# Two of the four heads' memory keys made in the first steps of the self-attention, and the copies of its high parts issued behind the turned probabilities

## Chip, cores and metric

The kernel is a hand-scheduled program for one core of a Trainium2 chip. It uses the core's five engines and its 16 DMA engines: PE (TensorE, matrix products; PEld is its weight load), DVE (VectorE), ACT (ScalarE), POOL (GpSimd) and SP (SyncE, which here only issues DMAs). The metric is the device time of one execution in microseconds (us), as the median of the runs; every number below that has no unit beside it is in us.

## The reference

One decoder layer over 1024 positions of width 1024, with 256 memory tokens:

```
x <- LN(alpha*x + mixer(x))          mixer = [retention | spatial gating | latent attention] @ w_out
x <- LN(alpha*x + cross(x, mem))     4 heads of 128, 256 memory tokens
x <- LN(alpha*x + moe(x))            16 experts, top 2 of one group

def memory_cross_attention(x, mem, wq, wk, wv, wo):
    q = (x @ wq).reshape(b, s, 4, 128)
    k = (mem @ wk).reshape(b, 256, 4, 128)      # the memory keys: they do not depend on x
    v = (mem @ wv).reshape(b, 256, 4, 128)
    p = softmax(q k^T * 128 ** -0.5)
    return (p v).reshape(b, s, 512) @ wo
```

The self-attention inside the mixer has 8 heads of 96 (64 without position, 32 rotated), values of 64, a causal mask, and works on 1024 keys.

## The kernel before

The program is a row of phases, each a block in which every engine has its own hand-written list of instructions. Engines meet only through semaphores inside a block, and all of them wait for one another at its end. The phases are `project` (the input projection), `prepare` (retention, gating, keys and queries of the self-attention), `attend` (the self-attention), `mix_out` (output projection, first normalization, memory keys), `cross_attend`, `experts` and `overflow`. A float32 product on PE is issued as two passes, so 8 products of one memory-key head show as 16 records. Where precision is bought more cheaply, an operand is split into a high part (type f32r) and a rest, and three products of one pass replace the two passes: names with `_hi` and `_lo`.

**prepare** (L435 to L658) walks over 8 tiles of 128 positions. PE turns the latents of the next tile (`latents_T`, L454 to L461, whose last transpose raises `lat_t`) inside the tile before. SP has nothing to do in this block.

**attend** (L667 to L902) works on 48 units, listed in `units` (L681): for tiles 0 to 3 a unit is two heads of a tile (4 units for a tile), for tiles 4 to 7 it is one head (8 units for a tile). Each unit u goes through this chain:

- PE `scores(u)` (L727 to L740) into half u % 2 of the buffer `s_ps`. Tiles 0 to 2 use plain float32 (L735); tiles from SPLIT = 3 on use three products of high and low parts (L737 to L739).
- DVE adds the causal mask (L853) and takes the row maximum (L857, L859).
- ACT exponentiates into `prob` (L805, L808).
- PE `turn(u)` transposes the probabilities into `t_ps` (L748).
- DVE copies the first half of them to `prob_T` (L866), ACT the second half (L817).
- PE `values(u)` multiplies them with the values (L761).

PE's order is `scores(u)`, `values(u-2)`, `turn(u-1)` for each u (L765 to L771). ACT's order for each u is: an eventual copy of high parts, then the exponentials of u, then the `prob_T` copy of u-1. The copies of high parts are `keys_high` (L776 to L780, 1024 columns of `k_hi`) and `queries_high` (L782 to L785, `q_hi`). For tiles 0 to 3 they stand ahead of units 4, 5, 6, 8 and 9 (L787 to L792); later, those of tile i+1 stand ahead of the units of heads 2 and 4 of tile i (L793 to L797). POOL makes the low parts from them (`k_lo` L876 and L889, `q_lo` L881), and `scores` of the first unit of a tile waits for both (L732 to L733). DVE also ends the retention at the start of its step u = 2 (L838, L842), and the high parts of the keys wait for that, since they are put where the retention's inputs were.

SP in attend (L706 to L714) loads slices 6 and 7 of `w_out` at once into a place of their own (62 KiB), then writes zeros into two DRAM tables (44 stores), then loads slices 0 to 5 of `w_out` to 137 KiB as the low parts of the queries that lie there are done with.

**mix_out** (L909 to L1063) multiplies the mixed heads with `w_out`, in three products of high and low parts (L975 to L977), adds x and normalizes. ACT splits `w_out` at tile 1, after waiting for all eight slices (L992 to L994). When the last tile's product is out, the block ends like this. PE makes the memory keys of all four heads, 8 products of 128x256 for each (L980 to L986). ACT makes the high part of the query weights (L1003). DVE adds the last tile (L1033), takes its statistics (L1037, L1039), normalizes the last two tiles (L1021, L1022), makes the low part of the query weights (8 subtractions, L1045) and copies the keys of four heads out of PE's buffer into `xkT` (4 copies, L1048). Then the block ends, and **cross_attend** starts with transposes (L1172), the memory values (L1288), and the queries (L1183 to L1185).

```
            n = len(units)
            for u in range(n + 2):
                if u < n: scores(u)
                if 0 <= u - 2: values(u - 2)
                if 0 <= u - 1 < n: turn(u - 1)
```

Of the kernel before, what the change touches and what calls it, by code (L numbers as in the profile page):

```python
# [15 lines left out]
P = 128  # L16
# [44 lines left out]
W_OUT_EARLY = 6  # L61
# [338 lines left out]
def prepare(nc, k):  # L400
# [266 lines left out]
def attend(nc, k):  # L667
# [25 lines left out]
    ret_normed, ret_gated = k.sem("ret_normed"), k.sem("ret_gated")  # L693
    k_hi_made, q_hi_made, q_lo_made, k_lo_made, k_old_lo_made = (
# [3 lines left out]
    nc.clear_and_free_semaphores([s for s in k.used[:older] if s is not k.ret_rstd_ready])  # L698
    with nc.psum_tensor("s_ps", [P, 2, 2, 512], f32) as sps, \
# [5 lines left out]
        def _(sp):  # L705
            for s in range(W_OUT_EARLY, KD):  # L706
                sp.dma_start(k.w_out_raw[s], A["w_out"][s * P:(s + 1) * P, :]).then_inc(k.w_out_loaded, 16)
# [4 lines left out]
            for s in range(W_OUT_EARLY):  # L712
                sp.wait_ge(scored, units.index((s + 1, 0)))
                sp.dma_start(k.w_out_raw[s], A["w_out"][s * P:(s + 1) * P, :]).then_inc(k.w_out_loaded, 16)  # L714
# [7 lines left out]
        def _(pe):  # L722
            def scores(u):
                i = units[u][0]
                if u >= 2:
                    pe.wait_ge(exps, 2 * (u - 1))
                if i == SPLIT:  # L727
                    pe.wait_ge(k_old_lo_made, units[u][1] // 2 + 1)
# [35 lines left out]

            n = len(units)  # L765
            for u in range(n + 2):
                if u < n:
                    scores(u)
                if 0 <= u - 2:
                    values(u - 2)  # L770
                if 0 <= u - 1 < n:  # L771
                    turn(u - 1)

        @block.scalar
        def _(act):
            def keys_high(t):  # L776
                if t == 0:
                    act.wait_ge(ret_gated, 1)
                tok = slice(t * P, (t + 1) * P)
# [7 lines left out]
            early = {4: 0, 5: 1, 6: 2, 8: SPLIT}  # L787
            for u in range(len(units) + 1):
                if u in early:
                    keys_high(early[u])  # L790
                if u == 9:
                    queries_high(SPLIT)  # L792
                if u < len(units) and SPLIT <= units[u][0] < NT - 1:  # L793
                    if units[u][1] == 2:
                        keys_high(units[u][0] + 1)
                    if units[u][1] == 4:
                        queries_high(units[u][0] + 1)  # L797
# [13 lines left out]
                if u >= 1:  # L811
# [5 lines left out]
                    act.activation(probT[:, v % 2, 1, 0:(z - a) * P], tps[:, 1, 0:(z - a) * P], ACT.Copy).then_inc(pT_copied_act, 1)  # L817

# [86 lines left out]
def mix_out(nc, k):  # L905
# [26 lines left out]
    with nc.psum_tensor("mixT_ps", [P, 2, 2, 512], f32) as tps, \  # L932
# [19 lines left out]
        def _(pe):  # L952
# [29 lines left out]
            for u in range(XH):  # L982
# [1177 lines left out]
```

## Time and profile before

| | |
|---|---|
| median of 3 runs | 1040.03 us (1038.56 to 1045.7) |
| the profiled execution, its own time | 1042.29 us |
| its span, first to last instruction | 1040.5 us |
| busy PE / PEld / DVE / ACT / POOL | 94% / 81% / 58% / 35% / 22% |
| granted TensorE clock, mean | 0.98 of full speed |

The profile shows one execution. Busy time of PE is modelled and includes waits inside its pipeline, so the start times of its instructions are the better measure. Between the first and the last instruction lie 1040.5 us, and 1.8 us of the execution's own time lie around them. "xN" after an instruction is a run of N records merged; the bracket behind it is the idle time of the engine before it and what ended it.

### The profile page before, as it was taken

Reading aid. Unit: us, or ns where it says so; the run is one execution under the profiler, and the core shown is the slowest. Engines: PE = TensorE matmul, PEld = TensorE weight load, DVE = VectorE, ACT = ScalarE, POOL = GpSimd, SP = SyncE. Lnnn points to the kernel's source line nnn. Section 1 sums busy time; section 2 is a strip of 40 time slices with the busy share of each in tenths; the row PEclk is TensorE's granted clock in tenths of the full one; section 3 lists DMA queues with packets and bytes.
Section 4 is the critical chain, followed back from the end, with each engine's and each line's share of the span. In section 5 each row is a group of like instructions: output and inputs, shape, how many; then the busy total and the mean of one; then the engine's idle time right before and its main releaser. Section 6 shows DMA issues by size and latency. Waiting matters only on the chain. (4 is left out here: it accounts for less than half of the span.)

```text
span 1040.5 us, 15996 instructions
## 1 busy us (share of the span) xinstructions
PE 981.2 (94%) x5687; PEld 843.9 (81%) x5687; DVE 607.8 (58%) x1273; ACT 365.8 (35%) x749; POOL 225.2 (22%) x286
## 2 busy tenths in 40 slices
PE   7999999999899999899999999999899999999993
PEld 5898877676779999778885888888778988888882
DVE  6644340677666665544472455458546676767674
ACT  5122131434564444500013332331134444544441
POOL 0012100121061110012220000003334544333343
PEclk9999999999799999899999999999899999999997
DMA  8022010000798100460203200042688788989962
GB/s 331 17 82 81 1 62 1 1 2 1 290 412 321 38 2 2 161 243 1 81 0 124 81 1 1 1 153 108 238 253 278 260 302 291 310 292 316 318 247 85
DMA packets 63737, 150.49 MB, mean 145 GB/s; under 512 B 10304, under 2 KB 12608, under 8 KB 63680
## 3 DMA queue, kind: packets, MB, share of 16 engines
q1 hardware_dynamic: 54720, 132.77, 36.3%
q0 software_dynamic: 8960, 16.96, 4.4%
q8 instruction: 36, 0.59, 0.2%
q14 instruction: 21, 0.17, 0.1%
HBM read 109.46 MB, written 54.92 MB: 158 GB/s over the span
## 5 line engine op out<-in xcount | busy, mean ns | idle before, releaser
L1764 PEld LDWEIGHTS h_ps<-xgT,e_gate_up 128*128 128x128 f32 x1024 | 157.2, 193 | 4.6 <-issue 2.3
L1764 PE MATMUL h_ps<-xgT,e_gate_up 128*128 128x176 f32 x1024 | 158.6, 317 | 2.2 <-PEq L1753 2.2
L248 PE MATMUL unit_ps<-whi,xhi 128*128 128x512 f32 (+1 forms) x256 | 98.3, 384 | 9.6 <-DVE wlo L279 9.6
L249 PE MATMUL unit_ps<-wlo,xhi 128*128 128x512 f32 (+1 forms) x256 | 98.0, 383 | 0.0
L250 PE MATMUL unit_ps<-whi,xlo 128*128 128x512 f32 (+1 forms) x256 | 97.9, 382 | 0.0
L761 PEld LDWEIGHTS o_ps<-mla_v,prob_T 128*128 128x128 f32 x576 | 71.5, 196 | 10.0 <-issue 5.2
L761 PE MATMUL o_ps<-mla_v,prob_T 128*128 128x64 f32 x576 | 72.7, 277 | 4.2 <-ACT prob_T L817 4.2
L248 PEld LDWEIGHTS unit_ps<-whi,xhi 128*128 128x128 f32 x256 | 48.7, 190 | 18.1 <-DVE xlo L318 7.4
L1882 DVE SCALAR_TENSOR_TENSOR z<-y_ps,slot_weight,x_rows 128x512 f32<-128x512 f32 (+1 forms) x64 | 45.6, 746 | 19.5 <-PE y_ps L1778 12.1
L1828 ACT ACTIVATE ln_junk<-z,z_neg_mean 128x1024 f32<-128x1024 f32 (+1 forms) x32 | 36.8, 1150 | 54.8 <-DVE z_neg_mean L1887 54.3
L1776 PE MATMUL y_ps<-e_dn_hi,h_hi 128*128 128x512 f32 (+1 forms) x128 | 52.1, 407 | 4.1 <-DVE z L1882 4.1
L250 PEld LDWEIGHTS unit_ps<-whi,xlo 128*128 128x128 f32 x256 | 48.6, 190 | 7.7
L249 PEld LDWEIGHTS unit_ps<-wlo,xhi 128*128 128x128 f32 x256 | 48.6, 190 | 7.6
L975 PE MATMUL mix_acc<-wo_hi,mixT_hi 128*128 128x512 f32 x128 | 51.1, 399 | 3.4 <-DVE wo_lo L1027 2.1
L976 PE MATMUL mix_acc<-wo_lo,mixT_hi 128*128 128x512 f32 x128 | 50.6, 395 | 0.0
L977 PE MATMUL mix_acc<-wo_hi,mixT_lo 128*128 128x512 f32 x128 | 50.5, 395 | 0.0
L1778 PE MATMUL y_ps<-e_dn_hi,h_lo 128*128 128x512 f32 (+1 forms) x128 | 50.5, 395 | 0.0
L1777 PE MATMUL y_ps<-e_dn_lo,h_hi 128*128 128x512 f32 (+1 forms) x128 | 50.2, 392 | 0.0
L808 ACT ACTIVATE prob<-s_ps,neg_max 128x640 f32<-128x640 f32 (+3 forms) x32 | 30.5, 954 | 55.5 <-issue 53.9
L866 DVE COPY prob_T<-t_ps 128x512 f32<-128x512 f32 (+3 forms) x48 | 29.9, 624 | 25.1 <-PE t_ps L748 25.0
L1850 DVE SCALAR_TENSOR_TENSOR ln_out<-ln_tmp,z_rstd,ln_b 128x1024 f32<-128x1024 f32 (+1 forms) x34 | 42.0, 1277 | 4.3 <-POOL z_rstd L1730 4.3
L1733 POOL DMA_INDIRECT out<-ln_out,slot_ids x32 | 34.0, 1062 | 46.4 <-DVE ln_out L1850 41.5
(313 smaller groups left out, 2093.0 us busy)
## 6 DMA issues: line engine op xcount, KB each, us to landing
e_gate_up<-w_gu SPq DMA_DIRECT2D x16, 2048.0 KB, 11.7
e_down_raw<-w_dn SPq DMA_DIRECT2D x16, 1024.0 KB
slot_rows<-zeros SPq DMA_DIRECT2D x22, 522.0 KB, 7.1
slot_sums<-zeros SPq DMA_DIRECT2D x22, 512.0 KB, 7.3
x_rows<-slot_rows SPq DMA_DIRECT2D x16, 522.0 KB, 4.4
slot_sums<-z SPq DMA_DIRECT2D x16, 512.0 KB, 4.0
wraw<-w_in SPq DMA_DIRECT2D x24, 256.0 KB, 4.7
xraw<-xT SPq DMA_DIRECT2D x8, 512.0 KB, 7.1
```

The lines of the kernel that those rows point to most:

```text
L248: pe.matmul(o, hi, whi[:, s, 0:w], start=(s == 0), stop=False)
L249: pe.matmul(o, hi, wlo[:, s, 0:w], start=False, stop=False)
L250: last = pe.matmul(o, lo, whi[:, s, 0:w], start=False, stop=(s == KD - 1))
L761: last = pe.matmul(ops[:, i % 2, h * MV:(h + 1) * MV], probT[:, u % 2, j, (m - a) * P:(m - a + 1) * P], k.v[:, m, h * MV:(h + 1) * MV], st ...
L975: pe.matmul(o, hi, whi[:, s, c], start=(s == 0), stop=False)
L976: pe.matmul(o, hi, wlo[:, s, c], start=False, stop=False)
L977: last = pe.matmul(o, lo, whi[:, s, c], start=False, stop=(s == KD - 1))
L1764: end = pe.matmul(hps[:, m, gu * CAP:(gu + 1) * CAP], gate_up[:, b, s, w], xT[:, s, :], start=(s == 0), stop=(s == KD - 1))
L1776: pe.matmul(out, hi, dn_hi[:, b, w, :], start=(f == 0), stop=False)
L1777: pe.matmul(out, hi, dn_lo[:, b, w, :], start=False, stop=False)
L1778: return pe.matmul(out, lo, dn_hi[:, b, w, :], start=False, stop=(f == 1))
L1882: dve.scalar_tensor_tensor(z[c][:, f], yps[r, BANK[u], :], wgt[r, b, c:c + 1], rows[b][r, c, f], ALU.mult, ALU.add, accum_out=zsum[r, c, j ...
```

## The change

- Head 0 and head 1 of the memory keys are made in attend: PE's list starts with `scores(0)`, `early_keys(0)`, `turn(0)`, `scores(1)`, `early_keys(1)`, `values(0)`, `turn(1)`, `scores(2)`, and goes on in the old order from u = 3 (where `scores(3)` comes first). ACT copies each result to `xkT`. `scores(1)` and `scores(2)` wait for these copies.
- Their inputs (1 MB of `memT`, two 512 KB column blocks of `xa_wk`) are loaded by SP in prepare, once the latents of the last tile are turned.
- mix_out makes and copies heads 2 and 3 only. It still loads all of `memT` and `xa_wk`.
- In attend, ACT's copies of high parts stand behind the exponentials and the `prob_T` copy of their step. For tiles 0 to 3 the step is one less than before; for the later ones it is the same step.
- All slices of `w_out` go to 137 KiB, slices 6 and 7 too; slice 7 is loaded when all scores are done. `xkT` is moved to another address.

```
-W_OUT_EARLY = 6
+KEYS_EARLY = 2
...
+        @block.sync
+        def _(sp):
+            sp.wait_ge(lat_t, NT)
+            sp.dma_start(k.mem_early[:], A["memT"].rearrange("(s p) n -> p s n", p=P)).then_inc(k.early_loaded, 16)
+            wk = A["xa_wk"].rearrange("(s p) n -> p s n", p=P)
+            for h in range(KEYS_EARLY):
+                sp.dma_start(k.wk_early[h][:], wk[:, :, h * XD:(h + 1) * XD]).then_inc(k.early_loaded, 16)
...
-            for s in range(W_OUT_EARLY, KD):
-                sp.dma_start(k.w_out_raw[s], A["w_out"][s * P:(s + 1) * P, :]).then_inc(k.w_out_loaded, 16)
...
-            for s in range(W_OUT_EARLY):
-                sp.wait_ge(scored, units.index((s + 1, 0)))
+            for s in range(KD):
+                sp.wait_ge(scored, units.index((s + 1, 0)) if s + 1 < NT else len(units))
...
+                if 1 <= u <= KEYS_EARLY:
+                    pe.wait_ge(keys_taken, u)
+            def early_keys(h):
+                if h == 0:
+                    pe.wait_ge(k.early_loaded, 16 * (1 + KEYS_EARLY))
+                else:
+                    pe.wait_ge(exps, 2 * h)
+                for s in range(KD):
+                    last = pe.matmul(sps[:, 1 - h, 0, 0:MEM], k.wk_early[h][:, s, :], k.mem_early[:, s, :], start=(s == 0), stop=(s == KD - 1))
+                last.then_inc(keys_sum, 1)
-            for u in range(n + 2):
+            scores(0)
+            early_keys(0)
+            turn(0)
+            scores(1)
+            early_keys(1)
+            values(0)
+            turn(1)
+            scores(2)
+            for u in range(3, n + 2):
...
                 if t == 0:
                     act.wait_ge(ret_gated, 1)
+                    act.wait_ge(keys_taken, KEYS_EARLY)
-            early = {4: 0, 5: 1, 6: 2, 8: SPLIT}
+            early = {3: 0, 4: 1, 5: 2, 7: SPLIT}
             for u in range(len(units) + 1):
-                if u in early:
-                    keys_high(early[u])
-                if u == 9:
-                    queries_high(SPLIT)
-                if u < len(units) and SPLIT <= units[u][0] < NT - 1:
...
+                if u < KEYS_EARLY:
+                    act.wait_ge(keys_sum, u + 1)
+                    act.activation(k.xkT[:, u, :], sps[:, 1 - u, 0, 0:MEM], ACT.Copy).then_inc(keys_taken, 1)
+                if u in early:
+                    keys_high(early[u])
+                if u == 8:
+                    queries_high(SPLIT)
+                if u < len(units) and SPLIT <= units[u][0] < NT - 1:
...
...
-            for u in range(XH):
+            for u in range(KEYS_EARLY, XH):
```

## Rows read from the trace of the kernel before

**Rows 1.** The page's part 1: busy time, share, instructions.
```profile
PE 981.2 (94%) x5687; PEld 843.9 (81%) x5687; DVE 607.8 (58%) x1273; ACT 365.8 (35%) x749; POOL 225.2 (22%) x286
```
**Rows 2.** Windows: stretch, length, busy PE PEld DVE ACT POOL, PEclk, DMA share, GB/s.
```profile
265.30:268.70 3.40, 1.16 (x9) 1.00 (x9) 1.91 (x5) 1.44 (x6) 1.27 (x2) 0.98 0.42 128
268.70:282.20 13.50, 12.85 (x49) 11.31 (x50) 6.70 (x18) 8.07 (x28) 0.00 (x0) 0.50 1.01 405
...
435.60:439.10 3.50, 3.50 (x11) 2.68 (x10) 3.50 (x4) 3.50 (x5) 0.00 (x0) 0.53 1.01 413
...
530.70:544.40 13.70, 13.70 (x65) 11.96 (x63) 12.70 (x17) 4.27 (x8) 2.71 (x2) 1.00 0.00 1
```
**Rows 3.** Timeline, end of mix_out and start of cross_attend.
```profile
530.73 13.97 PE L984 MATMUL mixT_ps<-memT,xa_wk_raw 128*128 128x256 f32 x64
...
531.00 1.22 DVE L1033 SCALAR_TENSOR_TENSOR x<-x,mix_acc 128x1024 f32<-128x1024 f32 x1 [5.70 <-PE mix_acc L977]
...
539.41 4.90 DVE L1045 TENSOR_TENSOR wq_lo<-wq_raw,wq_hi 128x512 fp32r<-128x512 f32 x8
544.24 1.41 DVE L1048 COPY xkT<-mixT_ps 128x256 f32<-128x256 f32 x4
...
545.95 1.06 PE L1172 MATMUL x_tps<-constants,x 128*128 128x128 f32 x8 [1.25 <-PEq L934]
...
546.85 7.03 PE L1288 MATMUL x_acc<-xa_wv_raw,memT 128*128 128x512 f32 x16
```
**Rows 4.** Timeline, end of prepare and first units of attend.
```profile
253.12 0.27 PE L461 MATMUL banks<-constants,kr 128*32 128x128 f32 x1
...
266.17 1.13 PE L735 MATMUL s_ps<-mla_kT,mla_qT 96*128 96x128 f32 x8 [1.30 <-PEq L450]
...
268.67 0.69 PE L748 MATMUL t_ps<-constants,prob 128*128 128x128 f32 x2 [1.38 <-ACT prob L805]
...
274.20 1.91 PE L735 MATMUL s_ps<-mla_kT,mla_qT 96*128 96x256 f32 x4
...
282.36 0.43 DVE L853 TENSOR_TENSOR s_ps<-s_ps,constants 128x256 f32<-128x256 f32 x1 [1.71 <-PE s_ps L735]
...
282.83 0.69 DVE L857 TENSOR_REDUCE neg_max<-s_ps 128x2 f32<-128x512 f32 x1
...
283.45 1.03 PE L735 MATMUL s_ps<-mla_kT,mla_qT 96*128 96x256 f32 x4
...
284.46 0.38 ACT L817 ACTIVATE prob_T<-t_ps 128x256 f32<-128x256 f32 x1
...
286.34 1.46 PE L735 MATMUL s_ps<-mla_kT,mla_qT 96*128 96x384 f32 x4
```
**Rows 5.** Timeline, end of attend and start of mix_out.
```profile
418.59 0.39 PE L739 MATMUL s_ps<-k_hi,q_lo 96*128 96x512 f32 x1
...
432.28 5.78 ACT L994 ACTIVATE wo_hi<-w_out_head 128x1024 fp32r<-128x1024 f32 x6
...
434.92 0.47 PE L975 MATMUL mix_acc<-wo_hi,mixT_hi 128*128 128x512 f32 x1 [2.14 <-DVE wo_lo L1027]
```
**Rows 6.** Timeline, the last units of tile 3.
```profile
307.70 1.05 ACT L785 ACTIVATE q_hi<-mla_qT 96x1024 fp32r<-96x1024 f32 x1
...
308.83 2.36 POOL L881 TENSOR_TENSOR q_lo<-mla_qT,q_hi 96x1024 fp32r<-96x1024 f32 x1 [1.06 <-ACT q_hi L785]
...
310.06 0.69 ACT L805 ACTIVATE prob<-s_ps,neg_max 128x512 f32<-128x512 f32 x1 [1.31 <-DVE neg_max L857]
...
311.40 0.59 ACT L817 ACTIVATE prob_T<-t_ps 128x512 f32<-128x512 f32 x1
...
314.74 0.48 PE L737 MATMUL s_ps<-k_hi,q_hi 96*128 96x512 f32 x1
```
**Rows 7.** DMA issues: x count, KB each, median us to landing.
```profile
w_out_head<-w_out SPq DMA_DIRECT2D x6, 512.0 KB, 7.7
...
memT<-memT SPq DMA_DIRECT2D x1, 1024.0 KB, 5.5
```

More of the change, by code:

```diff
@@ L696, in attend @@
     on, mv4, rs4, ret_ps = k.ret_last
-    nc.clear_and_free_semaphores([s for s in k.used[:older] if s is not k.ret_rstd_ready])
+    nc.clear_and_free_semaphores([s for s in k.used[:older] if s is not k.ret_rstd_ready and s is not k.early_loaded])
     with nc.psum_tensor("s_ps", [P, 2, 2, 512], f32) as sps, \
@@ L711, in _ @@
                 sp.dma_start(k.z_dram[t * P:(t + 1) * P, :], zeros[:, 0:D]).then_inc(k.rows_zeroed, 16)
[L712 to L714 removed]
+            for s in range(KD):
+                sp.wait_ge(scored, units.index((s + 1, 0)) if s + 1 < NT else len(units))
+                sp.dma_start(k.w_out_raw[:, s, :], A["w_out"][s * P:(s + 1) * P, :]).then_inc(k.w_out_loaded, 16)
         def parts(u):
@@ L763, in values @@
                 last.then_inc(pv_done, 1)
-            n = len(units)
-            for u in range(n + 2):
+            def early_keys(h):
[6 more added lines that the diff above has]
+                last.then_inc(keys_sum, 1)
+            n = len(units)
+            scores(0)
[7 more added lines that the diff above has]
+            for u in range(3, n + 2):
                 if u < n:
                     scores(u)
-                if 0 <= u - 2:
-                    values(u - 2)
-                if 0 <= u - 1 < n:
+                values(u - 2)
+                if u - 1 < n:
                     turn(u - 1)
@@ L817, in _ @@
                     act.activation(probT[:, v % 2, 1, 0:(z - a) * P], tps[:, 1, 0:(z - a) * P], ACT.Copy).then_inc(pT_copied_act, 1)
+                if u < KEYS_EARLY:
[6 more added lines that the diff above has]
+                if u < len(units) and SPLIT <= units[u][0] < NT - 1:
+                    if units[u][1] == 2:
+                        keys_high(units[u][0] + 1)
+                    if units[u][1] == 4:
+                        queries_high(units[u][0] + 1)
         @block.vector
@@ L993, in _ @@
                     for s in range(KD):
-                        act.activation(whi[:, s, :], wraw[s], ACT.Copy).then_inc(w_hi, 1)
+                        act.activation(whi[:, s, :], wraw[:, s, :], ACT.Copy).then_inc(w_hi, 1)
                 act.wait_ge(mix_t, t + 1)
@@ L1045, in _ @@
                 dve.tensor_tensor(k.wq_lo[:, s, :], rawq[:, s, :], k.wq_hi[:, s, :].bitcast(f32), ALU.subtract)
-            for u in range(XH):
-                dve.wait_ge(keys_sum, u + 1)
+            for u in range(KEYS_EARLY, XH):
+                dve.wait_ge(keys_sum, u - KEYS_EARLY + 1)
                 dve.tensor_copy(k.xkT[:, u, :], tps[:, u // 2, u % 2, 0:MEM])
@@ L2076, in program @@
     k.v = at("mla_v", 169, [P, NT, MW])
-    k.w_out_tail, k.w_out_loaded = at("w_out_tail", 62, [P, KD - W_OUT_EARLY, D]), k.sem("w_out_loaded")
-    w_out_head = at("w_out_head", 137, [P, W_OUT_EARLY, D])
-    k.w_out_raw = [w_out_head[:, s, :] if s < W_OUT_EARLY else k.w_out_tail[:, s - W_OUT_EARLY, :] for s in range(KD)]
+    k.w_out_raw, k.w_out_loaded = at("w_out_raw", 137, [P, KD, D]), k.sem("w_out_loaded")
     k.wuq = at("w_uq", 192, [P, QR // P, MH * MQ])
@@ L2089, in program @@
     k.memT = at("memT", 73, [P, KD, MEM])
-    k.xkT, k.xv = at("xkT", 12, [P, XH, MEM]), at("xv", 16, [P, 2, XW])
+    k.xkT, k.xv = at("xkT", 6, [P, XH, MEM]), at("xv", 16, [P, 2, XW])
+    k.mem_early = at("mem_early", 60, [P, KD, MEM])
+    k.wk_early = [at(f"xa_wk_early{h}", (68, 52)[h], [P, KD, XD]) for h in range(KEYS_EARLY)]
+    k.early_loaded = k.sem("early_loaded")
     k.xs_dram = nc.dram_tensor("slot_rows", [SLOTS, ROW], f32).ap()
```

7 lines of the change are left out of this document (2 added, 5 removed).

## The prediction, made before any run of the change

> **What bounds the kernel now.** I read the page's busy shares first: PE is busy for 94% of the span, every other engine for 58% or less [rows 1]. So PE's list is the thing to shorten, and a product that is moved from one place to another gains only if PE has idle time in the new place and is what the old place waits for. The average can't say that, so I went to the two places: the windows for clock and busy time [rows 2], then the timeline of both [rows 3, 4].
>
> The old place is the end of mix_out [rows 3]. The last product with `w_out` is out at about 530.9. From there two engines work side by side until the block ends. PE makes the keys of four heads: 64 records from 530.73, the last one's end at 544.70. DVE adds, normalizes, makes the low part of the query weights until 544.31 (539.41 + 4.90) and copies four keys until 545.65 (544.24 + 1.41). In 13.7 us DVE is busy for 12.70 [rows 2], and its four copies start back to back with no wait before them. So PE and DVE end together, and PE's keys are not alone in setting the end. The reader is to see that 7 us less of PE's work leave 14.3 us of DVE's list as they are.
>
> The new place is the start of attend [rows 4]. PE idles for 1.30 before the first scores (the change of blocks) and for 1.38 before the first `turn`, which waits for mask, maximum and exponentials of unit 0. The granted clock tells something else about this place: full until 268.7, then 0.50, the lower of the two levels (1.2 against 2.4 GHz), until 282.2 [rows 2]. The same four passes of 128x256 scores take 1.91 at 274.20 and 1.03 at 283.45 [rows 4]. PE had 1.16 busy us in the 3.4 before the clock fell [rows 2].
>
> **The change part by part.**
>
> *Keys taken out of mix_out.* Two heads are 32 of 64 records: 13.97 / 2 = 7.0 off PE's list, which then ends at about 537.7. DVE loses two of four copies, (1.41 - 0.41) / 3 = 0.33 apart (0.41 is one copy, taken from this line's own duration), so 0.67. DVE ends at 544.98 instead of 545.65, and the block with it. Gain: 0.7. Cover: DVE's chain from 531.0 to 544.31 (12.70 busy of 13.70), and it doesn't hang on PE's keys. Bounds: 0.7 if DVE stays the last, 7.0 if it were not there.
>
> *What the idle PE then costs.* PE stands still from 537.7 to 545.3, 7.6 us, and has dense work from 545.95: 1.06 of transposes, then 16 records of the memory values, which are the way to the queries [rows 3]. I take what followed the idle time before 434.92, 2.14 of it: the clock was at 0.53 from 435.6 to 439.1 though PE was busy for all of it [rows 2, 5]. Half of 3.5 us is lost there, 1.7. Here I take 1.5, since the transposes in front count for less. Bounds: 0, and 3.5 if two such stretches follow.
> The Trainium skill speaks against this part of the change: "TensorE: Matmul & The Clock Gate", section "What's actually happening", says that throttled is the default state and that activity releases it. By that rule a PE with nothing to do is not free, and the keys at the end also served to keep the clock up. The row at 434.92 agrees; no row shows the end of mix_out with an idle PE. Without the rule's effect the sum would be 1.5 lower.
>
> *Keys put into attend.* Each head costs 3.5 on PE at full clock (13.97 / 4). I follow the units by the durations of rows 4 at full clock. `scores(0)` is done at 266.7. Keys 0 run to 270.2. The softmax of unit 0 (268.6) lies under them, so the 1.38 of idle time before the first `turn` is used. Then `turn(0)`; ACT copies key 0 (0.38, as the 128x256 copy at 284.46), `scores(1)` waits for that and starts at about 270.85 (0.25 idle). Keys 1 run from 271.4 to 274.9, and the softmax of unit 1 and the end of the retention on DVE lie under them. `values(0)`, `turn(1)`, `scores(2)` to 276.3, `scores(3)` to 276.8. Now PE's order bites: `values(1)` stands behind `scores(3)` but needs ACT's `prob_T` copy of unit 1, which ACT makes after the exponentials of unit 2, and those need `scores(2)` of just before. Mask and maximum to 277.25, exponentials to 278.1, copy to 278.4: PE idles for 1.7. `scores(4)` starts at 279.15, where it was 274.20: 4.95 late.
> Then the steps run at full clock where they ran at half. At full clock a step is held by the chain scores, maximum, exponentials, `prob_T` copy, not by PE: 2.89 from 283.45 to 286.34. At half clock the four steps from 274.20 to 286.34 took 12.14, of which the last two were in part already at full clock. At full clock I take two steps as one turn of the chain: mask and maximum 1.15, two exponentials with their reads 1.3, copy 0.38, `values`, `turn` and `scores` on PE 2.0, handovers 0.2: 5.0, so 10.0 for four, and 1.0 for the `k_hi` copies of 1.05 that come in the way of exponentials: 11.0. So the lateness at `scores(8)` is 4.95 - 1.2 = 3.8. From there on the chain before and after is the same, and nothing in attend waits for a fixed time that could take it back: the zero stores have SP's queue to themselves and POOL's work hangs on the scores.
> Cost: 3.8. Bounds: 2.0 (all idle time in the first steps used, 1.38 + 1.3, and 2.3 from the clock) and 11 (below).
>
> *Clock in the new place.* I take it that the clock stays up: in place of 1.16 busy us in the stretch ahead of 268.7 PE would have about 2.5 of them, and dense ones. If it falls all the same, the keys are themselves the dense work that brought it back at 439.1 after 3.5 us.
>
> *Copies of high parts moved on ACT.* For tiles 0 to 3 "behind the copy of step u" and "ahead of step u + 1" is the same place in ACT's list, so nothing changes. For tiles 3 to 6 each copy of 1.05 moves from the front of its step to the back. It delayed nothing in front: ACT still idled before the next exponentials (1.31 before 310.06, behind the `q_hi` of 307.70) [rows 6]; so nothing is gained. What is late next is POOL's low part of the queries of tile 4. A tile of two-head units has only two steps between the copy and the next tile: now ACT does exponentials from 310.06, the `prob_T` copy until 311.99, then `q_hi` to 313.05; POOL needs 2.36 [rows 6], done at 315.45, where `scores` of tile 4 starts at 314.74. Stall: 0.7; the steps after it may take back some, as far as PE waits in them. I take 0.5. Later tiles have four steps between, and no stall. Bounds: 0 and 0.8.
>
> *Loads.* The latents of the last tile are turned at 253.4 [rows 4]. SP, idle in prepare, then issues three loads. `memT` with 1024 rows of 1 KB took 5.5 [rows 7]; two blocks of 1024 rows of 512 bytes lie between half of that and all of it each. One after the other the three are in at 264.4 to 269.9, and they overlap in part, since 5.5 holds the time to start too; the keys want them at 266.7. I cost this at nothing. The cover is the last tile of prepare (253.4 to 266.17); if it is gone, the keys start up to 3.2 late.
> The Trainium skill bears on this: "DMA: Bandwidth & Descriptors", section "Specifications", puts the smallest transfer for full rate at 512 bytes, which these rows just reach; no row of this case has that size. By it the loads come in early in the interval, and the sum is the same; only the chance of a late load is smaller.
> Slice 7 of `w_out` is now issued when the last scores are done, at 419.0, and takes 7.7 at most like its neighbours [rows 5, 7]: 426.7. ACT wants it at 432.28. Slack 5.6, cost nothing. The two 512 KB loads taken from the front of SP's list in attend don't bring the zero stores forward, as these wait for a memset. ACT's two key copies (0.38 each) are short, and only `scores(1)` waits for one with nothing else to do (the 0.25 above).
>
> **The sum.** 3.8 + 0.5 - 0.7 + 1.5 = 5.1 slower. The profiled execution had 1042.29 (span 1040.5), which gives 1047.4; against the median of the runs, 1040.03, it gives 1045.1, and this is my forecast. A measurement of this kernel can tell about 1% from no change (10.4 us), so half a per cent is "the same".
>
> **The rivals.**
> 1. *The clock stays down in the early steps* (slower side). The change of blocks leaves 1.30 idle, and PE's gaps behind keys 0 and keys 1 (0.25, 1.7) are like those that came with the fall at 268.7. Then both heads cost double, 7.0 more, and the later steps gain nothing back, 1.2 less: 1045.1 + 8.2 = 1053.3. It decides from the point where the clock is at half before keys 1 start. For it: 13.5 us at half clock now in this very place. Against: dense work ended the other low stretch within 3.5 us.
> 2. *The end of mix_out really gains* (faster side). If DVE's list were shorter than it looks, or its rows waited for PE in a way the profile hides, 7.0 would come off instead of 0.7, and with no idle PE there no clock is lost: 1045.1 - 6.3 - 1.5 = 1037.3. Against: DVE is busy for 12.70 of 13.70 there.
> 3. *The early keys cost little.* They fill idle time of the softmax chain at lower cost than I find (2.0 instead of 3.8), and the clock at the end holds: 1045.1 - 1.8 - 1.5 = 1041.8.
> 4. *The change doesn't find its inputs*: the loads come late, PE idles in front of keys 0 for up to 3.2, and the clock falls on that: 3.2 + 1.7, 1050.0.
>
> **How the numbers follow.** Forecast 0.55, rival 1 0.14, rival 2 0.07, rival 3 0.17, rival 4 0.07. The forecast's own range is 1041 to 1049 (its bounds and a run-to-run spread of some us). To hold 8 of 10 the range takes in rivals 3 and 4 and reaches to rival 1: 1038 to 1053. Over 1% slower is above 1050.4: most of rival 1 and a little of the rest, 0.13. Over 1% faster is below 1029.6: no case reaches it, 0.02. Same: 0.85.
>
> **What would show it.** In the changed profile: DVE's subtractions of `wq_lo` still end some 14.3 after the last tile's product, and the block ends 0.7 sooner than now by that count, with PE idle for about 7 us before the transposes of cross_attend. The granted clock is below full in the first 3 to 4 us of the memory values. In attend the keys are 16 records each, 0.22 apart, and the clock is at full through 268 to 282; `scores(3)` is followed by an idle PE until ACT's copy of unit 1; the first `scores` of tile 3 comes about 3.8 later than now; at the first unit of tile 4 PE waits for `q_lo`. Wrong would be: keys 0.43 apart, keys waiting for a DMA, a DVE that idles before `xkT`, or an attend that is not longer than now.

## The result and the profile after

The change costs about half a per cent: 1047.12 us in the median of 20 runs (1043.41 to 1053.1) against 1041.55 (1037.91 to 1047.89) for the kernel before, run beside it. The ratio is 1.0045, with a 95% interval of 1.0029 to 1.006; that is 4.7 us slower (the two medians are 5.6 apart), where the forecast was 5.1, and it lies within the 1% that the prediction called "the same". Of all the runs behind this document one is left out of its ratio, a run of e1 that took 1187 us at a granted clock of 0.80.

The profiled execution of after is the slowest of its 20, with an own time of 1053.1 (span 1051.0). So the stages are compared one by one, and only those that the change touches are put down to it. I cut the span at starts of products on PE, read from the timelines:

```
stage (from .. to)                                    before    after    difference
A  first scores .. first scores of tile 3              33.00    37.21      +4.21
B  .. last scores (tiles 3 to 7)                      119.42   119.69      +0.27
C  .. first product with w_out                         16.33    16.33       0.00
D  .. last product with w_out                          95.58    95.31      -0.27
E  .. first transposes of cross_attend                 15.45    14.80      -0.65
F  .. first query product                               7.37    10.35      +2.98
G  .. end of cross_attend's work, start of placement  178.35   178.19      -0.16
H  .. first expert product                             17.31    16.54      -0.77
   .. end of the span (experts)                       291.52   296.08      +4.56
```

A, B, E and F are where the change works, and they hold 6.8. The 4.56 in the experts is not the change's: the profiles of the ten experiments, which leave the experts as they are, have from 287.0 to 293.5 there with no relation to their edit. What makes that part vary is open. G ends, and H begins, at PE's second group of placement products (`x_qps<-selected_b`). The page's first part says little, as before [rows 1]: PE's busy time and its count of records are the same, since the products have only moved.

```profile
PE 982.1 (93%) x5687; PEld 841.3 (80%) x5687; DVE 607.4 (58%) x1271; ACT 366.8 (35%) x751; POOL 225.8 (21%) x286
```

The windows say more (stretch, length, busy PE, PEld, DVE, ACT, POOL, granted clock, DMA share, GB/s). The first four are the start of attend and answer to the first two of [rows 2]; the last three are the end of mix_out with PE busy, then with PE idle, and the start of cross_attend.

```profile
265.30:268.70 3.40, 2.20 (x12) 2.05 (x13) 1.47 (x3) 1.42 (x5) 1.61 (x2) 1.00 0.00 0
268.00:279.00 11.00, 9.11 (x53) 7.78 (x52) 4.41 (x14) 4.05 (x19) 0.12 (x1) 1.00 0.93 379
279.20:286.00 6.80, 6.80 (x27) 5.80 (x26) 3.16 (x7) 4.23 (x12) 0.00 (x0) 0.52 1.02 418
286.30:304.00 17.70, 16.58 (x110) 13.23 (x109) 11.87 (x22) 11.08 (x32) 11.52 (x6) 1.00 1.02 412
...
535.30:542.40 7.10, 7.04 (x33) 5.86 (x31) 6.23 (x7) 4.27 (x8) 2.71 (x2) 1.00 0.00 0
542.40:549.50 7.10, 0.00 (x0) 0.00 (x0) 7.03 (x12) 0.00 (x0) 0.00 (x0) 0.73 0.00 1
549.80:556.20 6.40, 6.36 (x14) 3.68 (x15) 1.23 (x1) 1.02 (x1) 1.01 (x7) 0.52 0.84 301
```

Before, 13.5 us at the start of attend were at half clock. Now the clock is full through both keys, and half only from 279.2 to about 286. At the end of mix_out PE is idle for 7.1 us in which DVE is busy for 7.03: DVE's list is what the block still has to wait for. The 6.4 us behind the change of blocks are at half clock.

The timeline of after at the start of attend (start, duration, engine, line, operation, out<-in, shape, records; in the bracket the idle time before it and what ended it), beside [rows 4]:

```profile
266.50 0.68 PE L744 MATMUL s_ps<-mla_kT,mla_qT 96*128 96x128 f32 x4 [1.31 <-PEq L450]
...
267.02 3.62 PE L781 MATMUL s_ps<-mem_early,xa_wk_early 128*128 128x256 f32 x16
...
271.11 0.71 PE L744 MATMUL s_ps<-mla_kT,mla_qT 96*128 96x128 f32 x4 [0.26 <-ACT xkT L838]
...
271.66 3.62 PE L781 MATMUL s_ps<-mem_early,xa_wk_early 128*128 128x256 f32 x16
...
275.84 1.13 PE L744 MATMUL s_ps<-mla_kT,mla_qT 96*128 96x128 f32 x8
...
278.61 0.63 PE L770 MATMUL o_ps<-mla_v,prob_T 128*128 128x64 f32 x4 [1.64 <-ACT prob_T L835]
...
279.30 1.79 PE L744 MATMUL s_ps<-mla_kT,mla_qT 96*128 96x256 f32 x4
...
303.71 0.47 PE L746 MATMUL s_ps<-k_hi,q_hi 96*128 96x512 f32 x1
```

The keys start 0.5 behind the first scores with no wait for a load, and 16 records take 3.62, 0.22 apart. There are two gaps, 0.26 for ACT's copy of key 0 and 1.64 in front of `values(1)`, and behind the second the scores take 1.79 instead of 1.03: that is half clock.

The end of mix_out and the start of cross_attend in after, beside [rows 3]:

```profile
535.27 7.07 PE L1014 MATMUL mixT_ps<-memT,xa_wk_raw 128*128 128x256 f32 x32
...
535.55 1.22 DVE L1063 SCALAR_TENSOR_TENSOR x<-x,mix_acc 128x1024 f32<-128x1024 f32 x1 [5.70 <-PE mix_acc L1007]
...
543.97 4.91 DVE L1075 TENSOR_TENSOR wq_lo<-wq_raw,wq_hi 128x512 fp32r<-128x512 f32 x8
...
548.79 0.75 DVE L1078 COPY xkT<-mixT_ps 128x256 f32<-128x256 f32 x2
...
549.84 1.94 PE L1202 MATMUL x_tps<-constants,x 128*128 128x128 f32 x8 [7.50 <-PEq L964]
...
551.57 9.19 PE L1318 MATMUL x_acc<-xa_wv_raw,memT 128*128 128x512 f32 x16
...
560.19 0.80 PE L1213 MATMUL x_qps<-wq_hi,x1T_hi 128*128 128x512 f32 x1
```

From DVE's addition to the end of its list are 13.99 us (549.54 - 535.55); before there were 14.65. PE has stood idle for 7.50 before the transposes, which then take 1.94 instead of 1.06, and the memory values 9.19 instead of 7.03.

### The profile page after: what moved, and what is told of

It is laid out like the page before. It is cut to its first block and busy times, and to the rows that moved or that the text cites. A ratio compares the mean times of both kernels' runs of the same rounds, so it can differ in the third digit from the quotient of the medians.

```text
span 1051.0 us, 16001 instructions
## 1 busy us (share of the span) xinstructions
PE 982.1 (93%) x5687; PEld 841.3 (80%) x5687; DVE 607.4 (58%) x1271; ACT 366.8 (35%) x751; POOL 225.8 (21%) x286
## 5 line engine op out<-in xcount | busy, mean ns | idle before, releaser
L1794 PEld LDWEIGHTS h_ps<-xgT,e_gate_up 128*128 128x128 f32 x1024 | 154.7, 191 | 4.7 <-issue 2.5
L1794 PE MATMUL h_ps<-xgT,e_gate_up 128*128 128x176 f32 x1024 | 156.1, 313 | 2.2 <-issue 2.2
```

The lines of the kernel that those rows point to most:

```text
L1794: end = pe.matmul(hps[:, m, gu * CAP:(gu + 1) * CAP], gate_up[:, b, s, w], xT[:, s, :], start=(s == 0), stop=(s == KD - 1))
```

## The experiments

Each ran beside the kernel before on the same chip, 12 runs in five rounds; e1 to e4, e5 to e8, and e9 with e10 ran on three different chips, so only the ratios to the kernel before can be compared, not the times. Differences to after are differences of such ratios, each known to 2 or 3 us, so that 1 or 2 us between two kernels are not told apart by time. Where the time can't tell, the stage lengths of the profiles help, in single executions. They scatter too wherever the clock falls in one execution and not in another, by 1 or 2 us, so a stage length counts only where rows of the timeline explain it:

```
kernel                    ratio [95%]               A      B      E      F      G     own time
before                                            33.00  119.42  15.45   7.37  178.35  1042.29
after                     1.0045 [1.0029,1.0060]  37.21  119.69  14.80  10.35  178.19  1053.10
e1_tail_short             1.0005 [0.9979,1.0030]  32.30  119.39  15.46  10.07  178.20  1038.62
e2_tail_filled            1.0012 [0.9988,1.0037]  37.20  119.77  14.79   7.37  179.92  1042.78
e3_copies_in_front        1.0048 [1.0028,1.0068]  35.20  119.36  14.79   8.96  178.61  1045.59
e4_keys_behind_scores2    1.0022 [1.0000,1.0043]  33.39  119.80  14.79  10.14  177.39  1042.27
e5_values_in_tail         1.0008 [0.9987,1.0029]  36.14  119.75  15.09   3.44  177.31  1036.46
e6_all                    0.9987 [0.9961,1.0013]  33.39  119.40  15.09   3.44  179.92  1039.22
e7_pool_takes_half        1.0055 [1.0032,1.0077]  35.19  119.78  16.20   9.94  176.17  1045.99
e8_only_copies_moved      1.0004 [0.9980,1.0028]  34.25  119.79  15.46   7.37  177.65  1039.81
e9_values_split           0.9965 [0.9940,0.9990]  33.38  119.38  15.09   3.43  175.21  1034.94
e10_tail_empty            0.9993 [0.9975,1.0011]  32.89  119.44  14.93   9.09  177.64  1036.60
```

**e1_tail_short: only the removal.** In before, mix_out's PE makes heads 2 and 3 alone.

```
-            for u in range(XH):
+            for u in range(2, XH):
                 for s in range(KD):
                     last = pe.matmul(tps[:, u // 2, u % 2, 0:MEM], ...
...
-                dve.wait_ge(keys_sum, u + 1)
-                dve.tensor_copy(k.xkT[:, u, :], tps[:, u // 2, u % 2, 0:MEM])
+                dve.wait_ge(keys_sum, u % 2 + 1)
+                dve.tensor_copy(k.xkT[:, u, :], tps[:, 1, u % 2, 0:MEM])
```

> The kernel before, with PE's products for memory keys 0 and 1 left out at the end of mix_out (32 of 64 records, 7.0 us of PE); DVE still makes four copies, of heads 2 and 3 twice, so the keys of heads 0 and 1 are not computed. Theory (DVE sets the end, and the idle PE loses clock): the block ends when it did, and the memory values behind it run partly at half clock, so 1.5 to 3 us slower than before. Rival (PE's products set the end): 6 to 7 us faster than before. Second rival (DVE sets the end, the idle time is free): no change, within 0.5 us.

Measured: 1039.7 against 1040.19, ratio 1.0005. That 7 us of PE's work at the end of mix_out are worth 7 is excluded (at most 2.2 faster); of the expected 1.5 to 3 slower the time shows nothing. Windows and timeline of e1:

```profile
536.00:544.00 8.00, 0.05 (x1) 0.00 (x0) 7.83 (x14) 0.00 (x0) 0.00 (x0) 0.72 0.00 1
544.20:551.00 6.80, 6.79 (x16) 3.96 (x17) 1.22 (x1) 1.02 (x1) 0.98 (x7) 0.59 0.85 308
```
```profile
542.49 1.41 DVE L1048 COPY xkT<-mixT_ps 128x256 f32<-128x256 f32 x4
...
544.21 1.94 PE L1172 MATMUL x_tps<-constants,x 128*128 128x128 f32 x8 [8.16 <-PEq L934]
```

DVE's list goes on as if nothing had been taken away: its four copies take the same 1.41, and the block ends with them (E 15.46, before 15.45). Behind the idle 8.16 the clock is at 0.59 and F is 2.70 longer. The time doesn't show these 2.7, which leaves open how much of a clock loss seen in a profile reaches the median; the interval allows it (up to +3.1).

**e10_tail_empty: all four heads out.** In before, no memory key is made at all; DVE copies raw weights in their place.

```
-            for u in range(XH):
-                for s in range(KD):
-                    last = pe.matmul(tps[:, u // 2, u % 2, 0:MEM], ...
-                last.then_inc(keys_sum, 1)
...
-                dve.tensor_copy(k.xkT[:, u, :], tps[:, u // 2, u % 2, 0:MEM])
+                dve.tensor_copy(k.xkT[:, u, :], k.wk[:, u, 0:MEM])
```

> The kernel before with all 64 records of the memory keys left out at the end of mix_out (14 us of PE); DVE copies four blocks of the raw weights in their place, so no memory key is computed. Theory (DVE's list of 14.8 us sets the end, and idle time costs one stretch of half clock however long it is): no faster than the kernel before, and up to 3 us slower; the block ends at most 0.5 us sooner after the last product with w_out. Rival (PE's products take part in setting the end): 7 to 14 us faster.

Measured: 1036.68 against 1037.7, ratio 0.9993. Fourteen us of PE's work are gone and nothing that can be measured is won. Timeline of e10:

```profile
531.04 1.22 DVE L1028 SCALAR_TENSOR_TENSOR x<-x,mix_acc 128x1024 f32<-128x1024 f32 x1 [5.70 <-PE mix_acc L977]
...
539.45 4.91 DVE L1040 TENSOR_TENSOR wq_lo<-wq_raw,wq_hi 128x512 fp32r<-128x512 f32 x8
...
544.27 0.90 DVE L1043 COPY xkT<-xa_wk_raw 128x256 f32<-128x256 f32 x4
...
545.47 1.94 PE L1167 MATMUL x_tps<-constants,x 128*128 128x128 f32 x8 [14.54 <-PEq L934]
```

DVE's rows are those of [rows 3] to within 0.04, only the copies are shorter (0.90 for 1.41), with a PE that has stood idle for 14.54. E is 0.52 shorter than in before, and the copies are 0.51 shorter. So PE's keys have no part in setting this end; DVE's list has, with one wait of 0.52 in it, for POOL's `ln_rs`. In the profile the shorter E and the longer F make 1.2 more than before; the interval of the time ends at +1.1.

**e2_tail_filled: the change, with PE busy in the old place.** In after, mix_out's PE makes all four heads; those of heads 0 and 1 are used by nobody.

```
-            for u in range(KEYS_EARLY, XH):
+            for u in (2, 3, 0, 1):
```

> The changed kernel, but PE makes all four heads' keys in mix_out too (heads 0 and 1 again, uncopied), so PE is busy until DVE is done. Theory: 7 us of useless products make it 1.5 to 3 us faster than the changed kernel, since the memory values stay at full clock; in the trace the first query product comes 7.4 us after the block's start as in the kernel before, not 10.4. Rival (the slow stretch in the changed profile is chance): the same as the changed kernel, or slower.

Measured: 1042.52 against 1040.19, ratio 1.0012. So 7 us of useless products seem to make after faster, by about 3.4 (1.0045 - 1.0012); the intervals overlap, and by them the 3.4 could be anything from about 0.5 to 6, so the profile has to carry it. Windows and timeline of e2:

```profile
549.00:552.00 3.00, 2.82 (x13) 1.89 (x14) 0.66 (x1) 1.02 (x1) 1.01 (x7) 1.00 0.52 178
```
```profile
549.18 1.06 PE L1202 MATMUL x_tps<-constants,x 128*128 128x128 f32 x8 [0.59 <-PEq L964]
```

The transposes take 1.06 again and F is 7.37 to the hundredth, as in before. (Not all of this profile speaks for e2. C, where its edit changes nothing, is 15.45 instead of 16.33, and G is 1.73 longer than in after, since products near its end run 0.43 apart instead of 0.23: the granted clock is 0.50 from 714.0 to 719.5.) Here the trace agrees with the Trainium skill, "TensorE: Matmul & The Clock Gate", section "What's actually happening", by which the throttled clock is the default and activity releases it. The price of an idle PE is in every profile that has one in front of the values: F is longer by 2.98 in after, 1.59 in e3, 2.77 in e4, 2.57 in e7, 2.70 in e1 and 1.72 in e10. In the time it may show here; in those of e1 and e10 it doesn't.

**e3_copies_in_front: the moved copies put back.** In after, ACT's `keys_high` and `queries_high` stand ahead of the exponentials again.

```
-            early = {3: 0, 4: 1, 5: 2, 7: SPLIT}
+            early = {4: 0, 5: 1, 6: 2, 8: SPLIT}
             for u in range(len(units) + 1):
+                if u in early:
+                    keys_high(early[u])
...
                 if u < len(units):
                     i, h = units[u]
```

> The changed kernel with ACT's copies of high parts back in front of the exponentials of their step. Theory: PE's wait for the low part of the queries at tile 4 (0.46 us in the changed profile) is gone, 0.3 to 0.7 us faster than the changed kernel, and nothing else moves. Rival (the move behind takes 1.05 us copies out of the way of exponentials, and is a gain): 0.5 to 2 us slower than the changed kernel.

**e8_only_copies_moved: the moved copies alone.** In before, the same blocks stand behind the `prob_T` copy.

```
-            early = {4: 0, 5: 1, 6: 2, 8: SPLIT}
+            early = {3: 0, 4: 1, 5: 2, 7: SPLIT}
...
                     act.activation(probT[:, v % 2, 1, 0:(z - a) * P], ...).then_inc(pT_copied_act, 1)
+                if u in early:
+                    keys_high(early[u])
...
```

> The kernel before with only ACT's copies of high parts moved behind their step. Theory: PE waits for the low part of the queries at tile 4, and the stretch from the first unit of tile 3 to the last scores is 0.3 us longer (119.7 instead of 119.4); the whole is within 0.5 us of the kernel before. Rival (moving them behind clears the way for exponentials): 0.5 to 2 us faster than before.

Measured: e3 1045.44 against 1040.19 (1.0048), e8 1037.9 against 1037.32 (1.0004). Neither time shows an effect. The profiles do: B is 119.69 to 119.80 in all six kernels whose copies stand behind, and 119.36 to 119.44 in all six whose copies stand in front. Rows of after, then of e8, at the first unit of tile 4, which answer to [rows 6]:

```profile
316.41 1.05 ACT L812 ACTIVATE q_hi<-mla_qT 96x1024 fp32r<-96x1024 f32 x1
...
317.54 2.35 POOL L911 TENSOR_TENSOR q_lo<-mla_qT,q_hi 96x1024 fp32r<-96x1024 f32 x1 [1.79 <-ACT q_hi L812]
...
319.99 0.47 PE L746 MATMUL s_ps<-k_hi,q_hi 96*128 96x512 f32 x1 [0.46 <-issue]
```
```profile
317.70 0.47 PE L737 MATMUL s_ps<-k_hi,q_hi 96*128 96x512 f32 x1 [0.47 <-issue]
```

POOL's low part ends at 319.89 and the scores start 0.10 later, behind 0.46 of idle time. That idle time is put down to "issue", but what ended just before it is POOL's row. e8 has the same gap, 0.11 behind the end of POOL's `q_lo`, and in e3 `q_lo` is done 3.5 ahead of these scores and there is no gap. So this part costs 0.3 to 0.4 in the profile.

**e4_keys_behind_scores2: another order of the first steps.** In after, key 1 is made behind `scores(2)` instead of in front of it, in a bank of `o_ps`, so that ACT's chain for unit 2 can start while PE makes it. For that bank to be free, DVE ends the retention one step earlier.

```
             scores(1)
+            scores(2)
             early_keys(1)
             values(0)
             turn(1)
-            scores(2)
...
-                    last = pe.matmul(sps[:, 1 - h, 0, 0:MEM], ...
+                    last = pe.matmul(sps[:, 1, 0, 0:MEM] if h == 0 else ops[:, 1, 0:MEM], ...
...
-                if u == 2:
+                if u == 1:
                     end_retention()
```

> The changed kernel with key 1 put behind scores(2) instead of ahead of values(0) and scores(2), in another PSUM bank, and the end of the retention one DVE step earlier. Theory (the idle 1.64 us of PE before values(1) comes from scores(2) being late, and the fall of the clock at 279 comes from that idle time): the idle time is gone and the clock stays up through the first units, 1.4 to 3 us faster than the changed kernel. Rival (the early steps are held by the two keys' 7 us of PE alone): within 0.5 us of the changed kernel.

Measured: 1042.15, ratio 1.0022, which is some 2.4 less than after; the intervals overlap. Windows and timeline of e4:

```profile
265.50:299.00 33.50, 31.53 (x195) 25.64 (x195) 20.07 (x44) 19.54 (x63) 12.24 (x7) 1.00 0.95 383
```
```profile
270.17 1.16 PE L744 MATMUL s_ps<-mla_kT,mla_qT 96*128 96x128 f32 x8 [0.26 <-ACT xkT L841]
...
271.17 3.62 PE L781 MATMUL o_ps<-mem_early,xa_wk_early 128*128 128x256 f32 x16
...
275.86 0.63 PE L770 MATMUL o_ps<-mla_v,prob_T 128*128 128x64 f32 x4
...
276.56 1.03 PE L744 MATMUL s_ps<-mla_kT,mla_qT 96*128 96x256 f32 x4
```

The gap of 1.64 is gone, the clock is full through all of A, and A is 33.39: two heads' keys for 0.4 more than before has without them. In the order of the change they are 2.2 above before at full clock (35.20 in e3) and 4.2 in after. The earlier end of the retention is not what gains here: in after DVE was done with it and then stood idle for 2.15 until unit 2's scores came.

```profile
276.56 0.43 DVE L883 TENSOR_TENSOR s_ps<-s_ps,constants 128x256 f32<-128x256 f32 x1 [2.15 <-PE s_ps L744]
```

The 1.8 between e3 and e4 compares two kernels at full clock. The 0.4 and the 2.2 don't: before had 13.5 us of half clock in A, and the kernels without early keys range from 32.30 (e1, at half clock for some 10 us) to 34.25 (e8, for over 16). Part of what makes the keys look cheap is that this low stretch is gone with them; no run shows A without keys at full clock.

**e5_values_in_tail: useful work in the emptied place.** In after, `memory_values(0)`, which stood between the first transposes and the first queries, is made at the end of mix_out, and ACT copies it there, where DVE copied it at the start of cross_attend.

```
@@ mix_out
+            pe.wait_ge(taken, NT - 1)
+            for s in range(KD):
+                last = pe.matmul(acc[:, 0, 0, :], memT[:, s, 0:P], k.wv[:, s, :], start=(s == 0), stop=(s == KD - 1))
...
+            act.activation(k.xv[:, 0, :], acc[:, 0, 0, :], ACT.Copy)
@@ cross_attend
             turn(0)
-            memory_values(0)
```

> The changed kernel with the first half of the memory values (16 records, 6.9 us of PE) moved from the start of cross_attend into PE's idle time at the end of mix_out; ACT copies them. Theory (PE was idle there for 7.5 us, and that idle time cost half-clock time behind it): the block ends about 0.6 us later than in the changed kernel, the first query product comes 3.5 us after the transposes instead of 10.4, and the kernel is 5 to 6 us faster than the changed one, about as fast as the one before. Rival (work in cross_attend's start is filler that hides ACT's and DVE's splitting of x, so moving it only opens a hole): at most 1 us faster than the changed kernel.

Measured: 1038.34 against 1037.32, ratio 1.0008: 3.8 less than after, where 5 to 6 were expected. F falls from 10.35 to 3.44, and E rises by 0.3. Part of the 6.9 in F isn't seen in the time. The hole of which the rival spoke is there too: PE waits 2.37 for DVE's low part of x in front of the first query product, as in e6 below.

**e6_all: e4, e5 and the copies in front together.**

> The values moved as in e5_values_in_tail, key 1 behind scores(2) as in e4_keys_behind_scores2, and ACT's copies in front as in e3_copies_in_front. If the parts add up: 4.2 us of the first units fall to 0.4, the 0.3 us of tile 4 are gone, the start of cross_attend is 3.9 us shorter than before: 3 to 4 us faster than the kernel before. Rival (the gains overlap, or the clock takes them back elsewhere): no faster than the kernel before.

Measured: 1036.79 against 1037.32, ratio 0.9987, an interval that holds no change. It was expected to win by 3 to 4; by the interval that is about the most that it can be. Windows and timeline of e6:

```profile
549.20:555.40 6.20, 6.17 (x15) 4.82 (x16) 0.00 (x0) 0.00 (x0) 0.00 (x0) 0.50 1.03 332
```

```profile
549.23 0.79 PE L1223 MATMUL x_qps<-wq_hi,x1T_hi 128*128 128x512 f32 x1 [2.37 <-DVE x1T_lo L1448]
...
549.82 0.63 PE L1224 MATMUL x_qps<-wq_lo,x1T_hi 128*128 128x512 f32 x1
```

With the values gone, nothing lies between the transposes and the queries: PE waits 2.37 for DVE's low part of x, and the queries behind it run 0.63 each, at half clock. The 24 products of the first tile's queries lie 8.23 from first to last start (549.23 to 557.46), against 5.64 in before; G is 179.92, 1.6 more than before. So moving the values filled one hole and opened another.

**e9_values_split: that gap filled too.** e6, with three of the eight steps of `memory_values(1)` taken from behind the queries and put into the gap.

```
-            def memory_values(m):
-                for s in range(KD):
+            def memory_values(m, steps):
+                for s in steps:
...
             turn(0)
+            memory_values(1, range(3))
```

> As e6_all, and three of the eight steps (6 of 16 records, 2.6 us) of the second half of the memory values pulled forward to stand between the first transposes and the first queries of cross_attend, where e6_all left PE idle for 2.37 us and the queries behind it ran at half clock. Theory (that idle time cost 1.5 to 1.7 us of half clock): the first queries come 0.2 us later after the transposes, at full clock, and the stretch up to the placement is 4 us shorter than in e6_all; 1.5 to 4 us faster than e6_all, 3 to 6 us faster than the kernel before. Rival (the second half of the values is needed as filler where it stood): no better than e6_all.

Measured: 1032.87 against 1037.7, ratio 0.9965, interval 0.994 to 0.999: 3.6 faster than the kernel before (between 1.0 and 6.2), and 2.3 faster than e6, whose interval overlaps. It is the only kernel here whose interval lies below that of after and below no change. Timeline of e9:

```profile
545.59 1.06 PE L1212 MATMUL x_tps<-constants,x 128*128 128x128 f32 x8 [0.93 <-PEq L968]
...
546.49 2.74 PE L1328 MATMUL x_acc<-xa_wv_raw,memT 128*128 128x512 f32 x6
...
549.02 0.50 PE L1223 MATMUL x_qps<-wq_hi,x1T_hi 128*128 128x512 f32 x1
```

Six records of 0.46 each fill the gap, the queries start at the same distance from the transposes (F 3.43), the first now 0.50 long, and the 24 products of the first tile lie 5.36 apart (549.02 to 554.38), 2.9 less than in e6. G is 175.21, 4.7 less than in e6; some 2.6 of that are the six records that now stand in F instead.

**e7_pool_takes_half: DVE's list shortened.** In after, four of the eight subtractions of `wq_lo` go to POOL.

```
-            for s in range(KD):
+            for s in range(KD // 2, KD):
                 dve.wait_ge(q_hi, s + 1)
                 dve.tensor_tensor(k.wq_lo[:, s, :], ...
...
+            for s in range(KD // 2):
+                pool.wait_ge(q_hi, s + 1)
+                pool.tensor_tensor(k.wq_lo[:, s, :], rawq[:, s, :], k.wq_hi[:, s, :].bitcast(f32), ALU.subtract)
```

> The changed kernel with four of the eight subtractions of the query weights' low part given from DVE to POOL at the end of mix_out. Theory (DVE's list sets the end of the block): the block ends 2 to 2.5 us sooner after the last product with w_out, and the kernel is 1.5 to 2.5 us faster than the changed one. Rival (something else holds the end, or POOL beside DVE slows both): less than 0.5 us.

Measured: 1044.84 against 1037.32, ratio 1.0055. The block ends 1.4 later than in after (E 16.20 against 14.80) instead of sooner. Timeline of e7:

```profile
538.35 7.33 POOL L1096 TENSOR_TENSOR wq_lo<-wq_raw,wq_hi 128x512 fp32r<-128x512 f32 x4
...
538.48 2.21 DVE L1051 SCALAR_TENSOR_TENSOR ln_tmp<-x,ln_mv,ln_g 128x1024 f32<-128x1024 f32 x1 [0.52 <-POOL ln_rs L1093]
...
542.93 4.50 DVE L1075 TENSOR_TENSOR wq_lo<-wq_raw,wq_hi 128x512 fp32r<-128x512 f32 x4
```

Each engine pays for the other. DVE's normalizing row takes 2.21, where it took 1.28 in after, and four subtractions take 4.50, where eight took 4.91. POOL needs 1.83 for each of its four; alone it took 2.35 for the 1024 columns of `q_lo` in after, from which an estimate for 512 is 1.18. The expected gain of 1.5 to 2.5 was missed because of this, and the miss says nothing against DVE's list as what sets the end: POOL is done at 545.68, DVE at 548.10, and PE's transposes start at 548.40, 0.30 behind DVE as in after.

```profile
547.36 0.74 DVE L1078 COPY xkT<-mixT_ps 128x256 f32<-128x256 f32 x2
```

## Why the prediction was right, step by step

**What bounds the two places: right.** DVE's list sets the end of mix_out. It predicted 0.7 from two fewer copies, and E is 0.65 shorter; the rows of e1 and e10 show DVE's list unmoved by a PE that has half or none of its products there.

**Keys in attend, 3.8: the mechanism held, the two parts of its size came out otherwise.** The start was followed to the tenth: the gap before `scores(1)` 0.26 (0.25 predicted), the gap before `values(1)` 1.64 (1.7), and `scores(4)` at 279.30 (279.15). The four steps from `scores(4)` to `scores(8)` were put at 11.0 at full clock, where before took 12.14; that was too slow. In e3, where the clock held, they took 9.56 (278.73 to 288.29), so 2.6 of the lateness came back, not 1.2. And "the clock stays up" failed in the profile of after, against the sign that the prediction had named for it: the clock fell behind that gap of 1.64, from 279.2 to 286, and the four steps took 11.57. Five profiles with the change's order of PE's first steps say how firm this is: in after, e2 and e5 the clock fell (A 37.21, 37.20, 36.14), in e3 and e7 it didn't (35.20, 35.19). So the term is 2.2 where the clock holds and 3.1 to 4.2 where it doesn't, and the 3.8 that was taken lies among the latter; it was too dear for the case that it described. The time of e2, which is nearly the keys alone (1.0012, at most +3.8), fits the 2.2 better than the 4.2.

**Idle PE, 1.5: the mechanism held, the size was at the low end; 3.0 in the profile of after, 1.6 to 2.8 in others.** It was taken from the stretch behind an idle 2.14, where half of 3.5 us was lost [rows 2, 5]. Behind 7.5 idle us the low clock held through the transposes and most of the values: 0.88 more on the transposes (1.94 for 1.06) and 2.16 on the values (9.19 for 7.03), together 3.0, near the upper bound of 3.5. Where the prediction saw the clock below full in the first 3 to 4 us of the values, it was so from the transposes on for 6.4. Behind the same idle 7.5, F is only 1.6 longer in e3 and 2.8 in e4 (2.6 in e7, behind 8.91), so the price differs from one execution to the next. e2 brings F back to 7.37; the times of e1 and e10 show no such price in before, so the median's share of it stays uncertain.

**Copies behind, 0.5: right, 0.3 in the profile.** The wait is where it was put, at the first unit of tile 4, for POOL's `q_lo`.

**Loads, slice 7, ACT's two copies: right, nothing.** No wait of PE for a load or of ACT shows, except the 0.26 that was foreseen. The keys start at 267.02 with no idle time, and ACT's first split of `w_out` waits for nothing. The issues in SP's list and that split, in after's timeline and in its DMA table (x count, KB each, median us to landing):

```profile
253.75 0.38 SPq L456 DMA_DIRECT2D mem_early<-memT  x1
...
254.18 2.26 SPq L459 DMA_DIRECT2D xa_wk_early<-xa_wk  x2
...
423.82 0.33 SPq L721 DMA_DIRECT2D w_out_raw<-w_out  x1
...
437.09 7.67 ACT L1024 ACTIVATE wo_hi<-w_out_raw 128x1024 fp32r<-128x1024 f32 x8
```
```profile
mem_early<-memT SPq DMA_DIRECT2D x1, 1024.0 KB, 5.4
...
xa_wk_early<-xa_wk SPq DMA_DIRECT2D x2, 512.0 KB, 6.7
...
w_out_raw<-w_out SPq DMA_DIRECT2D x8, 512.0 KB, 5.0
```

Issued by 256.4, the last block is in by about 263, some 4 us before it is wanted. Slice 7 is issued at 423.82 and wanted 13.3 later.

**The sum.** By the profile of after it is 4.2 + 0.3 - 0.65 + 3.0 = 6.8, where the clock falls in attend and the price behind the idle PE is at its highest; e3 and e7 put the first term at 2.2, and e3 the last at 1.6, which makes 3.5. The forecast was 3.8 + 0.5 - 0.7 + 1.5 = 5.1 and the runs say 4.7 (3.0 to 6.3). That 5.1 came so near is partly luck: a term too large for the clock that it assumed met one that was at the low end.

**The rivals.** The clock at half through the keys (1): no, 3.62 for a head; but it fell behind them in three of five profiles, which no rival had. A real gain at the end (2): no, by e1 and e10. Keys that cost little (3): not in the order of the change, but e4 shows that they can, 0.4. Late loads (4): no.

**What stays open.** Why the same list sometimes loses the clock behind the 1.64 gap; what the keys would cost in attend against a kernel that has full clock there without them; how much of the 3 us in F reaches the median when nothing else is changed; and the experts' scatter from 287 to 296 between single executions, which is larger than the effects studied here.

## What to carry to other kernels

A product moved off PE's list is worth what is late without it, and that is read from the other engines' lists at that place: here DVE ended there, so 7 and even 14 us of products were worth less than could be measured, and the idle PE that they left had a price of its own in the clock behind it (1.6 to 3.0 in the profiles). An emptied place on PE wants other work of the path (e5), and the gap which that leaves at its old place wants filling as well (e9); only then did the move pay. Where work goes into a chain of short steps, put it behind the instruction that starts the other engine's next link, not in front (1.8 less in A for the same keys, e4 against e3).

## What the runs showed of the hardware that was not expected

- **DVE and POOL slow each other.** `ln_tmp<-x,ln_mv,ln_g` took 1.28 in DVE's list in after and 2.21 beside POOL's subtractions, and DVE's own subtraction 1.13 (4.50 / 4) instead of 0.61 (4.91 / 8). The Trainium skill has the rule, "SBUF — State Buffer", section "Who interferes with whom": a DVE instruction with two inputs in SBUF contends with a GpSimd instruction that reads SBUF. The trace agrees: both DVE rows have two inputs in SBUF, and here both engines pay.
- **The length of a stretch at the low clock is not fixed.** At the start of attend it was about 14 us in before, some 10 in e1 (full again from 280) and over 16 in e8 (0.50 from about 271 past 286), with the same list on PE there. With the keys in it was 3 to 7 in the order of the change (after, e2, e5) or none (e3, e7), and none in the three kernels with key 1 behind `scores(2)` (e4, e6, e9).
